# First input-projection tile multiplied between the transposes of x, its weights loaded and split ahead of them

## What is computed

```
h    = RMSNorm(x)
proj = h @ w_in                      # q, k, v, z_attn, z_ssm, xBC, dt
attn = RMSNorm(dilated_attention(q, k, v)) * silu(z_attn)
ssm  = bidirectional SSD over conv(xBC) with dt, gated by silu(z_ssm)
y    = x + RMSNorm(concat(attn, ssm) @ w_out)
```

## Time and profile before

| | us |
|---|---|
| median of 3 runs | 2495.09 (2495.04 to 2497.39) |
| profiled execution | 2495.39 |
| its span, first to last instruction | 2493.4 |
| PE busy | 2463.2, 99% of the span |
| DVE busy | 1583.5, 64% |
| ACT busy | 909.4, 36% |
| mean granted PE clock | 0.996 of 2.4 GHz |

### The profile page before, as it was taken

One profiled execution on the slowest core, in us unless ns is written; L12 is line 12 of the kernel. 1 busy time (PEld: TensorE's weight loads), 2 busy tenths in 40 slices (PEclk: granted clock), 3 DMA queues, 4 the chain that ended last, 5 costly groups with the idle time before them and its releaser, 6 DMA issues.

```text
span 2493.4 us, 36615 instructions
## 1 busy us (share of the span) xinstructions
PE 2463.2 (99%) x13932; PEld 2331.3 (93%) x13932; DVE 1583.5 (64%) x2294; ACT 909.4 (36%) x1502; POOL 0.2 (0%) x4
## 2 busy tenths in 40 slices
PE   6999999999999999999999999999999999999998
PEld 5999999999999999999999999999999888888887
DVE  5447855555555555554888888888888654544447
ACT  5322333333333333333454454445445321211123
POOL 0000000000000000000000000000000000000000
PEclk9999999999999999999999999999999999999999
DMA  4332333333333333336444554564544322222225
GB/s 163 109 112 90 118 108 99 93 93 93 105 99 99 105 96 97 93 112 215 149 142 151 195 156 153 167 185 143 178 154 140 123 93 93 93 87 98 93 85 186
DMA packets 289728, 309.34 MB, mean 124 GB/s; under 512 B 14854, under 2 KB 232134, under 8 KB 286711
## 3 DMA queue, kind: packets, MB, share of 16 engines
q1 hardware_dynamic: 254375, 202.38, 26.4%
q10 hardware_dynamic: 35280, 106.03, 12.5%
HBM read 254.72 MB, written 60.98 MB: 127 GB/s over the span
## 4 chain that ended last, share of the span: by engine, by line
PE 86%; DVE 1%; issue 0%; ACT 0%; DVEq 0%; ACTq 0%
PE ps L828 33%; PE ps L625 23%; PE ps L901 20%; PE ps L786 2%; PE ps L753 2%; PE ps L720 2%; PE ps L736 1%; PE ps L796 1%; PE ps L760 0%; PE ps L727 0%; PE ps L809 0%; PE ps L769 0%; PE ps L910 0%; PE ps L951 0%; PE ps L745 0%
## 5 line engine op out<-in xcount | busy, mean ns | idle before, releaser
L828 PE MATMUL ps<-h_hi,w_hi 128*128 128x384 f32 x928 | 310.9, 335 | 0.0
L828 PE MATMUL ps<-h_hi,w_lo 128*128 128x384 f32 x928 | 310.6, 335 | 0.0
L828 PE MATMUL ps<-h_lo,w_hi 128*128 128x384 f32 x928 | 310.5, 335 | 0.0
L901 PE MATMUL ps<-h_hi 128*128 128x512 f32 x752 | 293.5, 390 | 0.0
L901 PE MATMUL ps<-h_lo,h_hi 128*128 128x512 f32 x752 | 292.6, 389 | 0.0
L901 PE MATMUL ps<-h_hi,h_lo 128*128 128x512 f32 x752 | 292.5, 389 | 0.0
L625 PE MATMUL ps<-h_hi,w_hi 128*128 128x384 f32 x1088 | 283.1, 341 | 0.0
L1840 DVE TENSOR_TENSOR w_lo<-raw_qk,w_hi 128x512 fp32r<-128x512 f32 x232 | 160.2, 691 | 192.8 <-ACT w_hi L1278 191.9
L625 PE MATMUL ps<-h_lo,w_hi 128*128 128x384 f32 x1088 | 277.1, 335 | 0.0
L625 PE MATMUL ps<-h_hi,w_lo 128*128 128x384 f32 x1088 | 277.0, 335 | 0.0
L988 ACT ACTIVATE w_hi<-w_raw 128x512 fp32r<-128x512 f32 x184 | 115.0, 629 | 428.4 <-PE ps L625 277.0
(11 more groups left out here) (248 smaller groups left out, 4208.5 us busy)
## 6 DMA issues: line engine op xcount, KB each, us to landing
w_raw<-in_w_in SPq DMA_DIRECT2D x184, 256.0 KB, 3.5
raw_qk<-in_w_in SPq DMA_DIRECT2D x87, 512.0 KB, 3.9
stage<-in_w_out SPq DMA_DIRECT2D x31, 1024.0 KB, 5.0
stage<-loc_scr ACTq DMA_DIRECT2D x16, 1536.0 KB, 6.8
stage<-zx_scr ACTq DMA_DIRECT2D x46, 384.0 KB, 8.5
stage<-in_w_in SPq DMA_DIRECT2D x29, 512.0 KB, 4.0
u_scr<-stage ACTq DMA_DIRECT2D x32, 384.0 KB, 2.6
zx_scr<-w_raw SPq DMA_DIRECT2D x29, 384.0 KB, 2.3
```

What stands on the lines that cost most here:

```text
L828: ins = nc.tensor.matmul(ps[:, bank, 0:HALF_T], w, h(k), start=(start and kk == 0 and q == 0), stop=(last and kk == KC - 1 and q == 2), sk ...
L901: last = nc.tensor.matmul(ps[:, bank, :], m[par][:, k * T + t * P:k * T + (t + 1) * P], w[slot][:, k * NBW:(k + 1) * NBW], start=(k == 0 a ...
```

## The change

The dt tile is no longer multiplied behind the transposes. Behind the transposes of block n, PE multiplies block n - 6 (`dt_block`: three matmuls of 384 columns, into PSUM bank 0 or 1 by half); the last six blocks follow the last transpose. Transposes now use 6 banks instead of 8 (`TURN = 6`). For this the dt weights are loaded right behind row tile 0 on SP's queue, ahead of `sq_c` and row tile 1, and split on ACT and DVE between row tiles 0 and 1; DVE now scales row tile 1 ahead of the copies of the parameter columns. A dummy square root of one element comes first on ACT. `biases_by_distance` follows the whole dt tile. The two `skip_cols` DMAs move from in front of ACT's block loop to behind it.

```diff
 X_TURNS = {8: 4, 12: 5}
-W_TURNS = {24: (0,), 27: (1,), 31: (2, 3)}
+TURN = 6
...
             load_x(0)
+            sp.wait_ge(w_zeroed, 1)
+            for c in range(NCH):
+                load_dt(c)
             sp.dma_start(sq_c[:, :], squares).then_inc(small_in, 16)
+            load_x(1)
...
-            for t in range(1, TT):
+            for t in range(2, TT):
                 load_x(t)
...
-            sp.wait_ge(w_zeroed, 1)
-            for c in range(NCH):
-                load_w(c, COL_DT, c, width=64)
...
+            def dt_block(n):
+                half, k = divmod(n, KT)
+                pe.wait_ge(h_lo_done, n + 1)
+                if n < NCH:
+                    pe.wait_ge(w_lo_done, NCH)
+                c, kk = divmod(k, KC)
+                w_h, w_l = (w[:, c, kk * P:(kk + 1) * P] for w in (w_hi, w_lo))
+                for p, (w, h) in enumerate(((w_h, h_hi), (w_h, h_lo), (w_l, h_hi))):
+                    last = nc.tensor.matmul(ps[:, half, 0:HALF_T], w,
+                                            h[:, k * T + half * HALF_T:k * T + (half + 1) * HALF_T],
+                                            start=(k == 0 and p == 0), stop=(k == KT - 1 and p == 2))
+                if half == 1 and kk == KC - 1:
+                    last.then_inc(tile_done if c == NCH - 1 else w_used, 1)
...
-                    if n >= 8:
-                        pe.wait_ge(h_lo_done, n - 7)
+                    if n >= TURN:
+                        pe.wait_ge(h_lo_done, n - TURN + 1)
...
-                        last = nc.tensor.transpose(ps[:, n % 8, q * P:(q + 1) * P],
+                        last = nc.tensor.transpose(ps[:, 2 + n % TURN, q * P:(q + 1) * P],
...
+                    if n >= TURN:
+                        dt_block(n - TURN)
+            for n in range(2 * KT - TURN, 2 * KT):
+                dt_block(n)
...
-            pe.wait_ge(h_lo_done, KT + 10)
-            for half in range(2):
-                gemm_half(0, 0, 0, half)
-                if half == 0:
-                    pe.wait_ge(h_lo_done, 2 * KT)
-                    biases_by_distance()
+            biases_by_distance()
             bc_tiles(0, None)
...
-            for t in range(4):
+            act.wait_ge(table_ones, 1)
+            nc.scalar.activation(cur[32:33, 121:122], table[32:33, 0:1], ACT.Sqrt)
+            root_of_x(0)
+            for c in range(NCH):
+                split_hi(c, c, 0)
+            for t in range(1, 4):
                 root_of_x(t)
-            for h in range(2):
-                act.dma_start(skip_cols[64 * h:64 * h + 64, :],
...
-                for c in W_TURNS.get(n, ()):
-                    split_hi(c, c, 0)
+            for h in range(2):
+                act.dma_start(skip_cols[64 * h:64 * h + 64, :],
...
             scale_x(0)
+            for c in range(NCH):
+                split_lo(c, c)
+            scale_x(1)
...
-            for t in range(1, 4):
+            for t in range(2, 4):
                 scale_x(t)
```

More of the change, by code:

```diff
@@ L366, in load_x, with load_dt @@
                 sp.dma_start(x_rows[t], src).then_inc(x_in[t], 16)
+            def load_dt(c):
+                src = w_rows[:, c * KC:(c + 1) * KC, COL_DT:COL_DT + 64]
+                sp.dma_start(w_raw[:, c, :].rearrange("p (k n) -> p k n", k=KC)[:, :, 0:64], src).then_inc(w_in_s[c], 16)
             load_x(0)
+            sp.wait_ge(w_zeroed, 1)
+            for c in range(NCH):
+                load_dt(c)
             sp.dma_start(sq_c[:, :], squares).then_inc(small_in, 16)
+            load_x(1)
             sp.dma_start(par_a, conv_w[0].rearrange("k (t p) -> (k t) p", p=P)).then_inc(small_in, 16)
@@ L376, in _, with load_w @@
                 r += n
-            for t in range(1, TT):
+            for t in range(2, TT):
                 load_x(t)
-            def load_w(n, col, c, width=P, waited=False, rows=None):
+            def load_w(n, col, c, rows=None):
                 k0 = (c if rows is None else rows) * KC
[L383 to L387, removed]
-            sp.wait_ge(w_zeroed, 1)
-            for c in range(NCH):
-                load_w(c, COL_DT, c, width=64)
+                src = w_rows[:, k0:k0 + KC, ds(col, P)]
+                sp.wait_ge(w_lo_done, n - NCH + 1)
+                sp.dma_start(w_raw[:, c, :].rearrange("p (k n) -> p k n", k=KC), src).then_inc(w_in_s[c], 16)
             sp.dma_start(table[0:32, :], rel_table).then_inc(hot_in, 16)
@@ L1014, in silu @@
                 nc.scalar.activation(dst[:, SEQ:T], src[:, SEQ + 4:T + 4], ACT.Silu).then_inc(done, 1)
-            for t in range(4):
+            act.wait_ge(table_ones, 1)
[4 more added lines that the diff above has]
+            for t in range(1, 4):
                 root_of_x(t)
-            for h in range(2):
-                act.dma_start(skip_cols[64 * h:64 * h + 64, :],
-                              d_skip[0].rearrange("(t h) -> h t", h=2)[h:h + 1, :].partition_broadcast(64)
-                              .rearrange("p a b -> p (a b)"), allow_slow_non_contiguous=True).then_inc(skip_in, 16)
             act.wait_ge(cols_read, 2)
@@ L1030, in _ @@
                 act.wait_ge(xt_done, n + 1)
-                nc.scalar.activation(h_hi[:, o:o + HALF_T], ps[:, n % 8, 0:HALF_T], ACT.Copy,
+                nc.scalar.activation(h_hi[:, o:o + HALF_T], ps[:, 2 + n % TURN, 0:HALF_T], ACT.Copy,
                                      scale=pre_cols[:, k:k + 1]).then_inc(h_hi_done, 1)
-                for c in W_TURNS.get(n, ()):
-                    split_hi(c, c, 0)
+            for h in range(2):
+                act.dma_start(skip_cols[64 * h:64 * h + 64, :],
+                              d_skip[0].rearrange("(t h) -> h t", h=2)[h:h + 1, :].partition_broadcast(64)
+                              .rearrange("p a b -> p (a b)"), allow_slow_non_contiguous=True).then_inc(skip_in, 16)
             def store_cb(g):
@@ L1483, in _ @@
                 dve.wait_ge(h_hi_done, n + 1)
-                nc.vector.scalar_tensor_tensor(h_lo[:, o:o + HALF_T], ps[:, n % 8, 0:HALF_T], pre_cols[:, k:k + 1],
+                nc.vector.scalar_tensor_tensor(h_lo[:, o:o + HALF_T], ps[:, 2 + n % TURN, 0:HALF_T], pre_cols[:, k:k + 1],
                                                h_hi[:, o:o + HALF_T].bitcast(f32), ALU.mult, ALU.subtract
                                                ).then_inc(h_lo_done, 1)
-                for c in W_TURNS.get(n, ()):
-                    split_lo(c, c)
             def biases_out():
```

## The result

The changed kernel takes 2504.27 us (median of 8 runs, 2502.96 to 2505.24), the kernel before 2495.18 beside it: ratio 1.0035, 95% interval 1.0024 to 1.0045. It is slower by about 9 us, a little beyond the 0.2% that can be told here. The forecast was 2501.7 with a range of 2487.5 to 2504.5: the measured median is inside by 0.2 us.

What follows compares the result with a forecast made beforehand. PE, busy 99% of the span, bounds the kernel; the head gives 6.6 us, but tile C starts 4.0 us late and the half clock costs 2.3: 2495.4 + 4.0 + 2.3 = 2501.7 us, range 2487.5 to 2504.5.

Steps and rivals of the forecast that it cites:

- x later: Head: dt chunks (2048 packets) ahead of x row tiles 1 to 5 make them land 1.9 us later; transposes start about 17.9.
- Transposes and pairs: Head: 18 transposes take 3.9 us, then PE-bound transpose and dt pairs; tile B at 50.5 instead of 57.1, gaining 6.6 us.
- The copies hold ScalarE: ACT's queue: 2080 small packets take 19.3 us, holding y_scr and strips until 76.9; tile C at 78.4, 4.0 us later.
- First packet: ACT's queue q10: 2.5 us from DMA issue to first packet, read from y_scr; with the skill's 0.6 us, time 2499.8.
- the first rival: ACT's queue: copies don't hold ACT, so only the head's gain counts: 2488.8 us; chance 0.18.
- Wait and clock: Before tile C: PE waits 10.7 us, then runs 5 us at the half clock, losing 2.3 us.

Runs made afterwards that it cites:

- e2: Kernel before with only the two skip_cols DMAs moved, directly in front of the y_scr DMAs on ACT: 2511.97 us, ratio 1.0072.
- e5: Changed kernel with one late copy of D in 128-byte pieces and strip copies cut into 7 blocks of 128 columns x 64 rows: 2488.78 us, ratio 0.9976.
- e1: Changed kernel with the two skip_cols DMAs put back in front of ACT's block loop: 2498.88 us, ratio 1.0021.
- e3: Changed kernel with D fetched late by one DMA in 128-byte pieces, halves picked by VectorE: 2498.75 us, ratio 1.0018.
- e10: e5 with the roots of x tiles 4 and 5 ahead of blocks 7 and 10, not 8 and 12: 2488.49 us, ratio 0.9972.
- e9: e5 with dt loads behind x's third tile, splits behind tile 2's scale, roots of tiles 3, 4, 5 ahead of blocks 6, 8, 10: 2487.72 us.

## Why the prediction was right, and where it was off

The cause held: the late copies keep ScalarE from tile C's splits, PE waits more than 11 us, and the 5 us that the head gives are more than used up. The time lies 2.6 us above the forecast, 0.3 above the forecast's own range (2498.5 to 2504) and 0.2 inside the whole one. Two of the eight runs lie outside it, so the last 0.2 us are luck. And one step was not as foreseen: the wait that ended last ran through SyncE's queue.

- **x later: mis-sized.** The 1.9 us were taken from the highest rate of small packets. Tile 2 was scaled at 17.83 and not at 14.74: 3.1 us. SyncE issues x tile 1 at 5.76 us, behind the four dt DMAs, and the dt packets share the engines with x tile 0. The transposes began at 19.17, 1.3 us later than said.
- **Transposes and pairs: right.** The first 19 took 4.32 us in all, each 421 ns long and overlapping the next, blocks follow 0.855 us apart (0.87 said), the wait before block 16 is 1.10 (1.2 said). Tile B starts at 52.09 instead of 50.5; the head gives 5.0 us instead of 6.6.
- **The copies hold ScalarE: right as to the cause, wrong as to the last wait.** The forecast let the queue hold ScalarE until the last strip, and said that a late brow store costs nothing as long as ScalarE is held. ScalarE was through both `y_scr` issues at 64.75, before the second copy had landed (68.8), and then waited 8.5 us for the brow store, until 73.23. The queue alone would have held the strips too: with the 7.8 us of e2 behind the second copy they would have been through at 76.6 at the earliest (an estimate; SyncE's loads ran beside them here), and they were at 79.63. That two different waits end within 3 us of each other is why the number came out near. The parts of the 2.8 us by which tile C is later than 78.4: the copies are issued at 46.73 and not 45.4 (+1.3); their first packets come 1.5 us behind the issue and not 2.5 (-1.0: none in 46:48, then 32 in 48:48.5); the second copy lands at 68.8, 20.6 us later and not 19.3 (+1.3, 101 packets in a us); from there to the last strip's issue it is 10.8 us and not 9.7 (+1.1): 4.4 until the brow store lands and 6.4 for the strips; 0.1 more for the splits.
- **First packet.** 1.5 us here, and in e5 `y_scr`, issued at 51.69, has its first packets in the window 51.5:53 and runs in full from 53: 1.3 us at most. In the kernel before, the 2.5 us were reckoned back from a rate; its trace has one packet of q10 already in 60.5:61, at most 2.2 us behind the issue at 58.85. The Trainium skill's 0.6 us (DMA: Bandwidth & Descriptors, Latency and other measured facts) is too low for these, but nearer than my 2.5. That page's rule on the order within one queue, on which the forecast rested against the first rival, agrees with this trace: `y_scr`'s megabytes flow only from 68, behind the copies.
- **Wait and clock: right.** 11.7 us (10.7 said), then 2.2 us lost to the half clock (2.3 said). The 5 us behind the 2.3 had one good source, the stretch after 30.32. The other, 99 to 104, is a part of a stretch of about 7 us (97 to 104) into which the clock fell while PE was busy.
- **What it missed:** the second cost behind the first. Had the first rival been true, 2488.8 would have been wrong by it: e1 and e3 show 2498.8 for that case. A rival's price was worked out from the head alone, although the head's gain moves `y_scr` and the strips ahead of loads that they used to follow.

## What to carry to other kernels

A DMA of a few KB in 4-byte pieces is not small: count its pieces, and ask what stands behind it on its queue and which engine's program stands behind that issue. When a step is made earlier, list the transfers that it now overtakes; the second cost here was an old transfer that had always come last and now came first. An idle stretch that ends in "issue" can hide a wait between two issues: take the lengths of the issues off first and see what is left. And once one wait is removed, read the whole list of waits again before adding gains up.

## What the runs showed of the hardware

- With ScalarE's queue full of 4-byte pieces, SyncE's queue moved nothing in the 18 us of window 48:66, though it had work from 49.67 on and the pieces took 4.5% of the engines' time. What was issued ahead of the pieces did move beside them: in e1, where ScalarE issued the copies at 19.47, q1 moved 944 packets in 24:26, of loads issued by 20.1, beside 404 of q10. Before, q1 moved 41 packets in 35:38, near the end of the copies. Idle engines are no sign that another queue can use them.
- An issue can last 8 us. A DMA of 1.5 MB was issued in 0.58 to 0.70 us where no copies stood ahead of it, in 7.95 behind them.
- The clock can fall without any wait. After tile C come narrow matmuls of 32 columns; in e5 PE is busy without a gap and the clock falls, in e10 it doesn't. Stretches 88:92 and 92:96 of e5:

```profile
88.00:92.00 4.00, 4.00 (x46) 3.80 (x40) 1.01 (x3) 3.95 (x6) 0.00 (x0) 1.00 0.48 133
92.00:96.00 4.00, 4.00 (x21) 4.00 (x21) 0.28 (x3) 1.87 (x4) 0.00 (x0) 0.54 0.42 94
```

and of e10, with the same sequence of matmuls (some 2 us earlier):

```profile
88.00:92.00 4.00, 4.00 (x37) 4.00 (x37) 0.84 (x2) 3.08 (x5) 0.00 (x0) 1.00 0.44 113
92.00:96.00 4.00, 4.00 (x24) 4.00 (x24) 1.11 (x8) 1.90 (x2) 0.00 (x0) 1.00 0.17 38
```

The half clock lasts from about 92 to 98.5 in e5 and is worth some 2.5 to 3 us (6.3 x 0.46 = 2.9); the kernel before and the changed one have it too, from about 97 to 104 and from 107 to 113. Of the ten runs of e5, the five whose mean granted clock is 0.999 took 2486.1 to 2488.3 us, the five at 0.998 took 2489.2 to 2491.2, the profiled one among them: a difference of the same size. Why the clock falls in one execution and not in another is not settled. This scatter is why single profiles of e5, e9 and e10 can't be ranked.
